# Prompt attention of a hybrid decoder step: TensorE's order of transposes and values product

## The chip, the cores and the metric

The kernel runs on one core of a Trainium2 chip. The metric is the time of one execution on the device in microseconds (us), from repeated runs. A profiled execution gives a trace of every instruction. The engines are TensorE (PE; PEld is its weight load), VectorE (DVE), ScalarE (ACT), GpSimd (POOL) and SyncE (SP); each works through its own instructions in order, and they wait for each other on semaphores.

## The reference

One inference step of a decoder layer. A prompt of 512 tokens and 8 sampled sequences of 8 tokens each, width 1024, go through a norm, one input projection, attention with 8 heads (2 key/value groups of 4 heads, head width 64) beside a pooling branch, an output projection and an MLP of width 4096. Everything is float32. Attention has three branches with their own keys and values: compressed blocks, selected blocks and a sliding window, mixed by gates. The part that this document is about is the prompt's:

```python
s = jnp.einsum('btgpd,bsgd->btgps', q, kv[..., 0, :]) * SCALE
s = s - slopes[None, None, :, :, None] * dist[None, :, None, None, :]
p = masked_softmax(s, mask)
o = jnp.einsum('btgps,bsgd->btgpd', p, kv[..., 1, :])
...
o = gates[0] * o_c + gates[1] * o_s + gates[2] * o_w
```

With 512 tokens in 8 blocks of 64, the 16 selected blocks are all blocks, so the selected branch is causal attention over the prompt, as is the window branch (window 512).

## The kernel before

The kernel is a sequence of blocks, each with one program per engine, and a block starts when the engines are through with the one before: projection and compression, prompt attention, attention of the samples, MLP. In the trace, prompt attention's main loop lies at about 247 to 332 us.

Prompt attention runs over 4 passes j, one for each head of a group (both groups' heads of that number are done together). A pass has U = 8 units: for each of 4 tiles of 128 queries, widest first, two branches (selected, window). A unit of tile i has scores of 128 queries against 128(i+1) keys, for two heads: widths of 512, 512, 384, 384, 256, 256, 128, 128. A unit goes through these stages:

- `scores` on TensorE (L1297) into two banks, two units in turn
- `sums` on VectorE (L1194): adds the distance penalty, takes the maximum, negates it (L1199)
- `exponent` on ScalarE (L1131), with the row sums
- `factors` on VectorE (L1204, L1208): one over the sum, times the gate
- the product with the factors on GpSimd (L1120); in the first two passes a page load for the samples' attention (L336) follows each of units 1 to 16
- `turn` on TensorE (L1312): 4(i+1) transposes of 64 rows into banks 4 and 5
- `keep_turned`: VectorE (L1212) copies bank 4 and ScalarE (L1137) copies bank 5 into a buffer `cpT`, of which there are two
- `values` on TensorE (L1327): 4(i+1) matmuls that add into bank 6; for the window branch, four more of the compressed branch (L1333)

Scores are issued AHEAD = 4 units before the values. The order on each engine is written out by hand in `body`. VectorE's step u is `keep_turned(u + 1)`, `sums(u + 4)`, `factors(u + 3)`; in steps 3 and 4 it also stages the next pass's queries (L1168) and penalties (L1173), and at a pass's end the factor of the compressed values (L1180), for which it waits until the pass's last values product is done. ScalarE's step is `keep_turned(u + 1)`, `exponent(u + 4)`, and at a pass's end a copy of bank 6 into `mixT` (L1145), for which the next pass's first values product waits.

`turn(u + 1)` waits for GpSimd's product of unit u + 1 and for both copies of unit u. `values(u)` waits for both copies of unit u. `scores(u + 4)` waits for the sums of unit u + 2.

Of the kernel before, what the change touches and what calls it, by code (L numbers as in the profile page):

```python
# [307 lines left out]
def const(m, name):  # L308
    a, n = m.ccols[name]
    return m.consts[:, a:a + n]  # L310
# [12 lines left out]
def values_at(m, i, br, n=P):  # L323
    return m.rowsT[0:n, i, KV * (br + 1) + P:KV * (br + 2)]
# [753 lines left out]
def prompt(nc, m, sems, sem):  # L1078
# [28 lines left out]
    with nc.Block() as block:  # L1107
        @block.sync
        def _(sp):
            for b in range(4):  # L1110
                load_window(sp, m, b, b, sems)
# [175 lines left out]
        @block.tensor  # L1287
        def _(pe):
            def scores(j, v):
                i, w = tile(v), width(v)  # L1290
                if v % U in (0, 4):
                    pe.wait_ge(q_staged, (j + v // U) * 2 + (1 + (v % U) // 4))
                if v >= 2:
                    pe.wait_ge(summed, j * U + (v - 1))
                for g in range(2):
                    a = HD * g
                    last = pe.matmul(pb[2 * (v % 2) + g][:, 0:w], m.qst[a:a + HD, P * i:P * i + P],  # L1297
                                     m.kT[a:a + HD, branch(v), 0:w], start=True, stop=True)
                last.then_inc(scored, 1)

            def turn(j, v):
                pe.wait_ge(scaled, j * U + (v + 1))
                if v >= 1:
                    pe.wait_ge(kept_dve, j * U + v)
                    pe.wait_ge(kept_act, j * U + v)
                n = tile(v) + 1
                for g in range(2):
                    for k in range(n):
                        to = 64 * (n * g + k)
                        for h in range(2):  # L1310
                            half = slice(64 * h, 64 * h + 64)
                            last = pe.transpose(pb[4 + h][:, to:to + 64], m.cp[v % 4][half, g, P * k:P * k + P],  # L1312
                                                ident[half, half])
                last.then_inc(p_turned, 1)

            def values(j, u):
                i, br = tile(u), branch(u)
                pe.wait_ge(kept_dve, j * U + (u + 1))
                pe.wait_ge(kept_act, j * U + (u + 1))
                if u == 0:  # L1320
                    pe.wait_ge(o_kept, j + 1)
                if u == 1:
                    pe.wait_ge(vst_staged, j + 1)
                out = lambda g: pb[6][HD * g:HD * g + HD, P * i:P * i + P]
                for k in range(i + 1):
                    for g in range(2):
                        last = pe.matmul(out(g), values_at(m, k, br)[:, HD * g:HD * g + HD],  # L1327
                                         m.cpT[u % 2][:, :, 64 * ((i + 1) * g + k):64 * ((i + 1) * g + k) + 64],
                                         start=(br == 0 and k == 0), stop=False,
                                         skip_group_check=True)  # L1330
                if br == 1:
                    for g in range(2):
                        last = pe.matmul(out(g), m.vst[0:64, HD * g:HD * g + HD], m.ccT[0:64, P * i:P * i + P],  # L1333
                                         start=False, stop=True, skip_group_check=True)
                if u == U - 1:
                    last.then_inc(o_done, 1)

            def body(j, last):
                for u in range(U):
                    values(j, u)  # L1340
                    if not last or u + 1 < U:
                        turn(j, u + 1)
                    if not last or u + AHEAD < U:
                        scores(j, u + AHEAD)

            scores(0, 0)
            scores(0, 1)
            pe.wait_ge(kc_ready, 1)
            for i in range(PTILES):
                for j in range(HPG):  # L1350
                    a = 64 * i + 16 * j
                    last = pe.matmul(pb[7][:, a:a + 16], m.qT[:, j, P * i:P * i + P], m.kc2, start=True, stop=True)
            last.then_inc(c_scored, 1)
            pe.matmul(pb[6][0:64, 0:P], const(m, "spread8")[0:PBLK, :], m.vc[0:PBLK, NB_SEQ, :], start=True, stop=True)\
              .then_inc(c_scored, 1)
            for v in range(2, AHEAD):
                scores(0, v)
            pe.wait_ge(c_ready, 2)
            for i in range(PTILES):
                last = pe.transpose(pb[7][0:64, P * i:P * i + P], m.cc[:, 64 * i:64 * i + 64], ident)  # L1360
            last.then_inc(c_turned, 1)
            pe.sem_inc(o_kept, 1)
            turn(0, 0)
            pe.wait_ge(vst_staged, 1)
            for j in range(HPG):
                body(j, j == HPG - 1)
# [746 lines left out]
```

## Time and profile before

| | us |
|---|---|
| median of three runs | 936.3 |
| lowest and highest | 934.24, 938.38 |
| profiled execution | 931.72 |
| its span, first to last instruction | 929.9 |
| mean granted TensorE clock, share of full | 0.953 |

The page gives the busy time of each engine over the span, a clock row in 40 slices of 23 us each, and groups of instructions with the idle time in front of them. Terms of a sum are taken from the profiled execution and compared with its own time.

### The profile page before, as it was taken

Reading aid. Unit: us, or ns where it says so; the run is one execution under the profiler, and the core shown is the slowest. Engines: PE = TensorE matmul, PEld = TensorE weight load, DVE = VectorE, ACT = ScalarE, POOL = GpSimd, SP = SyncE. Lnnn points to the kernel's source line nnn. Section 1 sums busy time; section 2 is a strip of 40 time slices with the busy share of each in tenths; the row PEclk is TensorE's granted clock in tenths of the full one; section 3 lists DMA queues with packets and bytes.
Section 4 is the critical chain, followed back from the end, with each engine's and each line's share of the span. In section 5 each row is a group of like instructions: output and inputs, shape, how many; then the busy total and the mean of one; then the engine's idle time right before and its main releaser. Section 6 shows DMA issues by size and latency. Waiting matters only on the chain.

```text
span 929.9 us, 16973 instructions
## 1 busy us (share of the span) xinstructions
PE 838.3 (90%) x7066; PEld 757.7 (81%) x7066; DVE 440.6 (47%) x971; ACT 334.5 (36%) x608; POOL 122.4 (13%) x119
## 2 busy tenths in 40 slices
PE   5999988877777787898899999999999999999994
PEld 4999966764544454566899999999999999999993
DVE  5335545645677756663535543244333442343324
ACT  6501054542355555453424441123211331133203
POOL 0000101100486424441020000000000000000000
PEclk8999999997699978999899999999999999999998
DMA  8912636841254020556420222222112222222002
GB/s 286 333 51 92 189 75 219 278 147 60 77 183 136 2 80 4 223 227 151 145 89 2 91 90 91 90 90 79 50 56 86 90 90 90 90 90 90 0 0 102
DMA packets 48782, 102.72 MB, mean 110 GB/s; under 512 B 7498, under 2 KB 19166, under 8 KB 46429
## 3 DMA queue, kind: packets, MB, share of 16 engines
q1 hardware_dynamic: 41821, 68.48, 22.2%
q0 software_dynamic: 6912, 33.56, 10.4%
q8 instruction: 35, 0.57, 0.3%
q14 instruction: 14, 0.11, 0.0%
HBM read 97.62 MB, written 8.53 MB: 114 GB/s over the span
## 4 chain that ended last, share of the span: by engine, by line
PE 50%; DVE 1%; ACT 1%; issue 0%; DVEq 0%; ACTq 0%
PE bank L1987 50%; DVE low L1974 1%; ACT low L1900 0%; DVE wl L1913 0%; PE bank L2029 0%; ACT wh L1856 0%; ACT small L1906 0%; DVE small L1971 0%; DVE hT L1926 0%; DVE hT L1951 0%; DVE xl L1930 0%; ACT low L1870 0%; DVE xl L1919 0%; ACT xh L1872 0%; DVEq L1810 0%
## 5 line engine op out<-in xcount | busy, mean ns | idle before, releaser
L1987 PE MATMUL bank<-xh,wh 128*128 128x288 f32 x640 | 138.2, 298 | 4.3 <-DVE xl L1919 3.9
L1987 PE MATMUL bank<-xl,wh 128*128 128x288 f32 x640 | 138.0, 297 | 0.0
L1987 PE MATMUL bank<-xh,wl 128*128 128x288 f32 x640 | 137.9, 297 | 0.0
L1856 ACT ACTIVATE wh<-low 128x1024 fp32r<-128x1024 f32 x72 | 75.1, 1050 | 121.3 <-PE bank L1987 121.0
L1987 PE MATMUL bank<-ah,wl 128*128 128x288 f32 x512 | 109.7, 296 | 0.0
L1987 PE MATMUL bank<-ah,wh 128*128 128x288 f32 x512 | 109.6, 296 | 0.0
L1987 PE MATMUL bank<-al,wh 128*128 128x288 f32 x512 | 109.6, 296 | 0.0
L1987 PEld LDWEIGHTS bank<-xh,wh 128*128 128x128 f32 x640 | 104.0, 190 | 5.0 <-DVE wl L1913 4.2
L1987 PEld LDWEIGHTS bank<-xl,wh 128*128 128x128 f32 x640 | 104.1, 190 | 0.0
L1987 PEld LDWEIGHTS bank<-xh,wl 128*128 128x128 f32 x640 | 103.9, 190 | 0.0
L1951 DVE TENSOR_TENSOR hT<-bank,hT 128x288 f32<-128x288 f32 x64 | 26.3, 453 | 138.9 <-PE bank L1987 138.9
L1913 DVE TENSOR_TENSOR wl<-low,wh 128x1024 fp32r<-128x1024 f32 x72 | 87.5, 1217 | 2.4 <-ACT wh L1856 2.4
L1987 PEld LDWEIGHTS bank<-ah,wh 128*128 128x128 f32 x512 | 82.5, 189 | 0.0
L1987 PEld LDWEIGHTS bank<-al,wh 128*128 128x128 f32 x512 | 82.5, 189 | 0.0
L1987 PEld LDWEIGHTS bank<-ah,wl 128*128 128x128 f32 x512 | 82.5, 189 | 0.0
L1883 ACT ACTIVATE tmp<-tmp 128x576 f32<-128x576 f32 x32 | 22.0, 686 | 152.2 <-DVE tmp L1947 152.2
L1947 DVE SCALAR_TENSOR_TENSOR tmp<-bank,norm 128x288 f32<-128x288 f32 x64 | 26.3, 454 | 103.6 <-PE bank L1987 103.4
L948 DVE TENSOR_TENSOR blkl<-bank,blkh 128x512 fp32r<-128x512 f32 x64 | 40.5, 684 | 25.3 <-ACT blkh L906 25.3
L1131 ACT ACTIVATE zone<-zone,small 128x512 f32<-128x512 f32 (+3 forms) x64 | 35.4, 554 | 41.9 <-DVE small L1199 40.5
L1327 PEld LDWEIGHTS bank<-zone,rowsT 128*64 128x64 f32 x320 | 18.4, 142 | 36.7 <-DVE zone L1212 29.3
L906 ACT ACTIVATE blkh<-bank 128x512 fp32r<-128x512 f32 x64 | 34.3, 597 | 34.5 <-PE bank L1012 34.5
L1327 PE MATMUL bank<-zone,rowsT 128*64 128x128 f32 x320 | 25.8, 290 | 23.1 <-ACT zone L1137 9.6
(323 smaller groups left out, 1375.2 us busy)
## 6 DMA issues: line engine op xcount, KB each, us to landing
low<-in_w_up SPq DMA_DIRECT2D x8, 2048.0 KB, 8.2
low<-in_w_down SPq DMA_DIRECT2D x8, 2048.0 KB, 7.8
zone<-in_cmp_w SPq DMA_DIRECT2D x16, 256.0 KB
o_swin<-in_state_win SPq DMA_DIRECT2D x8, 504.0 KB
px<-in_x_prompt SPq DMA_DIRECT2D x4, 512.0 KB, 5.4
u_raw<-in_w_in SPq DMA_DIRECT2D x1, 2048.0 KB, 10.0
q_raw<-in_w_in SPq DMA_DIRECT2D x1, 2048.0 KB, 10.4
low<-in_state_win SPq DMA_DIRECT2D x4, 512.0 KB
```

What stands on the lines that cost most here:

```text
L906: act.activation(m.blkh[u % RING][:, r, :], pb[4 + 2 * (u % 2) + r][:, :], ACT.Copy).then_inc(blk_hi, 1)
L948: dve.tensor_tensor(m.blkl[u % RING][:, r, :], pb[4 + 2 * (u % 2) + r][:, :], m.blkh[u % RING][:, r, :].bitcast(F32), ALU.subtract).then_i ...
L1131: last = act.activation(m.cp[v % 4][:, g, 0:width(v)], m.cp[v % 4][:, g, 0:width(v)], ACT.Exp, bias=nm(v)[:, g:g + 1], accum_out=su(v)[:, ...
L1327: last = pe.matmul(out(g), values_at(m, k, br)[:, HD * g:HD * g + HD], m.cpT[u % 2][:, :, 64 * ((i + 1) * g + k):64 * ((i + 1) * g + k) + 64],
L1856: act.activation(wcols(m.wh, i), raw_cols(i), ACT.Copy).then_inc(wh_ready, 1)
L1883: act.activation(m.act[i % 2], m.relu[i % 2], ACT.Square).then_inc(a_ready, 1)
L1913: dve.tensor_tensor(wcols(m.wl, i), raw_cols(i), wcols(m.wh, i).bitcast(F32), ALU.subtract)\
L1947: op = dve.scalar_tensor_tensor(out=half(m.relu[i % 2], hf), in0=out(i, hf), scalar=0.0, in1=half(m.rb, hf), op0=ALU.max, op1=ALU.mult)
L1951: op = dve.tensor_tensor(h, out(i, hf), h, ALU.add)
L1974: last = dve.scalar_tensor_tensor(out=m.yo[i][0:n, 512 * hf:512 * hf + 512], in0=pb[2 * (i % 4) + hf][0:n, :], scalar=yv(i)[0:n, :], in1=m ...
L1987: last = pe.matmul(out(i, hf), w[wi], half(x[:, k, :], hf), start=first and part == 0, stop=end and part == 2)
```

## The change

TensorE's step issues `turn(u + 1)` in front of `values(u)` where it issued it behind. The waits in both functions stay as they are; no other engine's program changes.

```diff
             def body(j, last):
                 for u in range(U):
-                    values(j, u)
                     if not last or u + 1 < U:
                         turn(j, u + 1)
+                    values(j, u)
                     if not last or u + AHEAD < U:
                         scores(j, u + AHEAD)
```

## Rows read from the trace of the kernel before

**Rows 1.** The page: span, busy time, and clock in 40 slices.
```profile
span 929.9 us, 16973 instructions
...
PE 838.3 (90%) x7066; PEld 757.7 (81%) x7066; DVE 440.6 (47%) x971; ACT 334.5 (36%) x608; POOL 122.4 (13%) x119
...
PEclk8999999997699978999899999999999999999998
```

**Rows 2.** Waits, 247 to 335 us: us in total, times, longest.
```profile
PEld bank L1327 <- DVE zone L1212: 29.3, 28, 1.8
POOL zone L1120 <- DVE small L1208: 28.6, 20, 4.8
...
DVE zone L1212 <- PE bank L1312: 17.4, 19, 3.1
```

**Rows 3.** A group by form, same stretch: busy us, mean ns | idle before.
```profile
L1327 PE MATMUL bank<-zone,rowsT 128*64 128x128 f32 x320 | 25.8, 290 | 23.1 <-ACT zone L1137 9.6 <-DVE zone L1212 8.0 <-ACT mixT L1145 3.0
```

**Rows 4.** One pass, values to values, by windows: length, then busy time.
```profile
293.53:315.45 21.92, 16.22 (x209) 10.12 (x209) 17.27 (x79) 12.88 (x41) 10.46 (x9) 1.00 0.04 17
```

**Rows 5.** Timeline of a step in mid-pass: start, us, instruction.
```profile
298.11 1.47 POOL L1120 TENSOR_TENSOR zone<-zone,small 128x768 f32<-128x768 f32 x1 [2.02 <-DVE small L1208]
...
299.45 0.88 PE L1327 MATMUL bank<-zone,rowsT 128*64 128x128 f32 x12 [0.19 <-DVE zone L1212]
...
300.26 0.59 PE L1312 MATMUL bank<-consts,zone 64*128 64x64 f32 x12
...
300.68 0.44 PE L1297 MATMUL bank<-kT,zone 64*128 64x128 f32 x4
...
300.89 0.56 DVE L1212 COPY zone<-bank 128x384 f32<-128x384 f32 x1 [0.23 <-PE bank L1312]
...
301.37 0.28 DVE L1194 CUSTOM_DVE_ANT_0 zone<-zone,bank 128x128 f32<-128x128 f32 x1
```

**Rows 6.** Timeline of the third boundary between passes.
```profile
311.08 1.89 POOL L1120 TENSOR_TENSOR zone<-zone,small 128x1024 f32<-128x1024 f32 x1 [1.73 <-DVE small L1208]
...
312.49 0.44 PE L1327 MATMUL bank<-zone,rowsT 128*64 128x128 f32 x4 [0.98 <-ACT zone L1137]
...
313.23 0.71 PE L1312 MATMUL bank<-consts,zone 64*128 64x64 f32 x16
...
313.77 0.86 PE L1297 MATMUL bank<-kT,zone 64*128 64x384 f32 x4
313.98 0.69 DVE L1212 COPY zone<-bank 128x512 f32<-128x512 f32 x1 [0.61 <-PE bank L1312]
...
314.70 0.55 DVE L1194 CUSTOM_DVE_ANT_0 zone<-zone,bank 128x384 f32<-128x384 f32 x1
```

**Rows 7.** Timeline of the first boundary: transposes and their copy.
```profile
268.45 0.72 PE L1312 MATMUL bank<-consts,zone 64*128 64x64 f32 x16
...
269.73 0.69 DVE L1212 COPY zone<-bank 128x512 f32<-128x512 f32 x1 [1.14 <-PE bank L1312]
```

**Rows 8.** Timeline of the last pass's end.
```profile
326.78 0.61 POOL L1120 TENSOR_TENSOR zone<-zone,small 128x256 f32<-128x256 f32 x1 [1.55 <-DVE small L1208]
...
327.77 0.66 PE L1327 MATMUL bank<-zone,rowsT 128*64 128x128 f32 x8 [0.80 <-ACT zone L1137]
327.83 0.61 POOL L1120 TENSOR_TENSOR zone<-zone,small 128x256 f32<-128x256 f32 x1 [0.43 <-DVE small L1208]
...
328.72 0.34 PE L1312 MATMUL bank<-consts,zone 64*128 64x64 f32 x4
...
329.10 0.29 DVE L1212 COPY zone<-bank 128x128 f32<-128x128 f32 x1 [1.35 <-PE bank L1312]
...
330.69 0.69 PE L1327 MATMUL bank<-zone,rowsT 128*64 128x128 f32 x4 [0.46 <-DVE zone L1212]
```

**Rows 9.** Timeline of the first step: transposes and their copy.
```profile
249.62 1.12 PE L1312 MATMUL bank<-consts,zone 64*128 64x64 f32 x16
...
250.78 0.69 DVE L1212 COPY zone<-bank 128x512 f32<-128x512 f32 x1 [3.12 <-PE bank L1312]
```

## The prediction
> **What bounds the kernel now.** I read the page first: one core, TensorE busy 90% of a 929.9 us span, and from about 500 us on nearly without a gap [rows 1]. The change touches only prompt attention, about 247 to 332 us. There the page's clock row, one digit to 23 us, shows the granted clock near its upper level with small dents. So next I asked for the waits of that stretch, engine by engine. TensorE's large wait is in front of the values product, L1327: its weight loads sat idle 29.3 us in 28 waits until VectorE's copy out of the transposes' banks (L1212) was done, and its matmuls 23.1 us [rows 2, 3]. VectorE in turn waited 17.4 us for the transposes. In this stretch no wait of TensorE was released by GpSimd: a product of GpSimd's (L1120) has always landed before its transposes get their turn. VectorE is busy 17.27 us of a 21.92 us pass [rows 4].
>
> I write, for one of the 32 units n: V(n) the values product, T(n) its transposes, K(n) the two copies, S(n) scores, X(n) VectorE's sums, F(n) the factors, E(n) ScalarE's exponent, P(n) GpSimd's product. Step n on TensorE is now V(n), T(n+1), S(n+4); on VectorE it is K(n+1), X(n+4), F(n+3), in that order. P(n+3) follows F(n+3).
>
> The timeline of one step in mid-pass is the key reading [rows 5]. Here n is 18. V(18) starts at 299.45, T(19) at 300.26, S(22) at 300.68 and ends at 301.12. K(19) starts at 300.89 and ends at 301.45; X(22) starts at 301.37. So the copy already runs beside the scores, and both end within 0.3 us of each other. The idle time in front of V is what is left of a ring: VectorE can't take X(n+4) before S(n+4) is done, and takes K(n+2) only after X(n+4) and F(n+3).
>
> **The change part by part.** Nothing is added or removed: the same 320 values matmuls (25.8 us) [rows 3], the matmuls of the compressed branch and the transposes are issued, with the same waits. T(n+1) moves in front of V(n). Both wait for K(n), so T can start where V starts now. No DMA and no queue of another engine is moved. V(n) and, behind it, S(n+4) now stand behind T(n+1), which also waits for P(n+1).
>
> 1) Middle of a pass. If P(n+1) is there, V and T swap places and S(n+4) starts when it does now. Only the copy is early, by the length of V. X(n+4) then starts after S instead of after K. For n = 18: S ends 301.12; X starts 0.06 later, as it does in [rows 6] (S 313.77 + 0.86 = 314.63, X 314.70), so at 301.18 instead of 301.37: a gain of 0.19 us. The next step, where both copies are narrower, gives some 0.06 by my reading; the steps of 512 and of narrow units around a pass's end give nothing, since X waits for S or for VectorE's own staging there. That is 0.25 us a pass, 1.0 us over four passes. The other bound is in the same rows: P(19) ends at 298.11 + 1.47 = 299.58, later than the 299.45 at which V(18) starts. Taking 0.1 us to see it, T(19) would start at 299.68, V(18) 0.42 later (T to S now), S another 0.81 later (V to T now), 300.91: ends 301.35, X 301.41, a loss of 0.04 us. If P also comes earlier, because its X did, the gain stands. I take the gain, and keep the loss for the range.
>
> 2) The boundary of two passes. Step 23 [rows 6]: V(23) starts at 312.49, T(24) at 313.23, S(27) at 313.77, X(27) at 314.70. P(24), the widest product, lands only at 311.08 + 1.89 = 312.97. T(24) can then start at 313.07, V(23) at 313.07 + 0.54 = 313.61, S(27) at 313.61 + 0.73 = 314.34. S starts 0.57 us later than now, and X(27), which starts at S's end even now, moves by 0.57 us. Behind it on VectorE stand F(26), the staging of the values factor and K(25), so the whole pass moves. At the two earlier boundaries GpSimd issues a page load behind each product, and the copy K starts 1.28 us after T (268.45 to 269.73) [rows 7] against 0.75 us here (313.23 to 313.98). This 0.53 us is a cushion: S may slip by it before it, not the copy, holds X. There I take 0.1 us each. The sum is 0.57 + 0.1 + 0.1 = 0.8 us lost. Bounds: 0.3 us if the gains of 1) bring P(24) forward too, 1.7 us if the cushion isn't one.
>
> 3) The end of the last pass, where there is no S left to hide a copy [rows 8]. Now: V(29) 327.77, T(30) 328.72, K(30) 329.10 to 329.39, V(30) 0.13 after that, 329.52, T(31) one short V later, 329.89, V(31) 330.69. Changed: T(30) starts at 327.77 (its product landed at 326.78 + 0.61 = 327.39) and takes some 0.20; V(29) runs 327.97 to 328.92; P(31) landed at 327.83 + 0.61 = 328.44, so T(31) starts at 328.92, V(30) at 329.12; K(31) starts 0.38 after T(31), as K(30) after T(30), and ends 329.59; V(31) starts at 329.72. That is 0.97 us earlier. A bound below is 0.5 us, if each copy's wait is only half hidden; above, 1.5 us, if V(31) also runs at the upper clock (0.44 instead of the 0.69 us of [rows 8], for it and for the pair behind it).
>
> The block after this one starts when all engines are through, so what is won or lost here reaches the end whole.
>
> Sum: -1.0 (1) + 0.8 (2) - 1.0 (3) = -1.2 us; since the loss of 1) is not unlikely I round it to -1.0. The profiled execution took 931.7 us beside its span of 929.9; it becomes 930.7. The median of the runs shown, 936.3, lies 4.6 above it; less 1.0 it is 935.3. No change is within 0.5%, 4.7 us, which is about what a measurement of this kernel can tell from none (the three runs span 934.24 to 938.38).
>
> **The rivals.**
>
> A: the copies are what bounds the pass. Then every wait of VectorE for the transposes goes, 17.4 us [rows 2] less the 3.1 us of the first one [rows 9], in which TensorE ran at its lower clock: 14 us, 922 us; half of it 929. For it: 28 of 28 waits in front of V name a copy. Against it: [rows 5], where scores end as the copy does, and VectorE's 17.27 us of work a pass, which leaves at most 4.65 us a pass whatever TensorE does. It needs X to start well before S ends, which it can't. The Trainium skill, Perfetto Trace Analysis, section Optimizing Tensor Performance, says that independent matmul groups should rotate through banks so that one group's evacuation lies beside the next group's matmuls; by that rule this order, which puts V between T and its copy's reader, should pay, and the time would be the 922 to 929 us of this rival. The trace bears it out only at the pass's end.
>
> B, slower: GpSimd's product becomes the wait in front of T, and holds V and S with it. Two steps of the ring S, X, F, P, T, S then have V(n) inside them, which now stands outside. Each step whose product lands later than K(n) by over about 0.1 us loses up to the length of V: 0.57 us at the boundary. Over the 28 steps that have scores, 0.2 us each is 5.6 us (941.9); 0.3 us is 8.4 (944.7). It decides from the point where products land 0.3 us later than now in most steps, for instance if GpSimd's signal reaches TensorE slower than VectorE's. For it: in [rows 5] the product is already 0.13 us behind. Against it: the gain in the same step offsets it, and GpSimd waits for VectorE 28.6 us [rows 2], so it isn't itself full.
>
> C: the clock. TensorE's order and its pauses change, so a stretch at 1.2 GHz could be longer or shorter. At the lower level sixteen transposes take 1.12 us [rows 9] against 0.71 [rows 6], and four values matmuls 0.69 [rows 8] against 0.44 [rows 6]; a step costs some 1.4 us more. Three steps either way are 4.2 us. For it: the clock falls right at the end of this part, at V(31). Against: the page's clock row shows nine tenths or more in the three slices from 256 to 325 us [rows 1], pauses and all.
>
> D: nothing moves at all, the gain of 3) included: 936.3.
>
> **How the numbers follow.** Forecast 0.64, A 0.11, B 0.12, C 0.08, D 0.05. Faster by over 0.5% is 0.8 of A and a quarter of C: 0.11. Slower by over 0.5% is 0.7 of B and a quarter of C: 0.10. Within: 0.79. The forecast's own range, from its bounds (-2.5 to +1.2 us) and 2 us of scatter, is 932 to 939. The range takes in the near halves of A to C: 930.5 to 940.
>
> **What would show it.** In the profile after: T(n+1) starts where V(n) started; the copies L1212 begin earlier against S, and TensorE's idle time in front of L1327 falls, to be found again in front of the transposes, L1312, with GpSimd named as releaser, above all at the boundaries. The pass lengths (22.6 and 21.9 us) stay within 0.3 us. The last three steps together are some 1 us shorter than now. The forecast is wrong if passes shorten by over 1 us (A), if T's waits for GpSimd sum to over 5 us beyond what V's waits lose (B), or if the clock row changes (C).

## The result, and the profile after

The changed kernel is slower. In the first comparison, 20 runs of each, its median is 938.5 us against 932.7 (ratio 1.0058, 95% interval 1.0035 to 1.0081); in a second, 12 runs against 35, it is 936.2 against 934.1 (1.0036, 0.9997 to 1.0075), which alone wouldn't tell it from no change. Medians are of all executions, ratios of those within 1.5% of the fastest of their kernel. The forecast was 1 us faster, within 0.5%.

The page of its profiled execution:

```profile
span 932.3 us, 16973 instructions
...
PE 841.7 (90%) x7066; PEld 757.9 (81%) x7066; DVE 440.4 (47%) x971; ACT 333.0 (36%) x608; POOL 122.6 (13%) x119
...
PEclk8999989988699998899799999999999999999998
```

The instruction counts are the same as in [rows 1]. The span says little here: two executions of the kernel before have spans of 929.9 and 935.8 us, because the stage ahead of prompt attention ends anywhere between 238 and 251 us and the samples' attention behind it takes 111 to 116 us, whatever is done in between. So I read all runs by a length inside the trace: **prompt attention**, from the start of its first copy L1212 to the start of the last copy L1145. Before it is 86.4 and 87.1 us in two profiles, changed 88.7 and 88.8. And within it by a middle pass, from one copy L1145 to the next, where the windows show the clock (third number from the end) at 1.00. Columns: window, length, then TensorE, its weight loads, VectorE, ScalarE, GpSimd. The kernel before, second profile:

```profile
273.38:295.94 22.56, 16.23 (x208) 10.12 (x208) 17.43 (x79) 13.16 (x43) 17.96 (x17) 1.00 0.56 187
295.94:318.25 22.31, 16.69 (x206) 10.75 (x208) 17.05 (x79) 13.00 (x43) 10.98 (x9) 0.95 0.06 23
```

The changed kernel, first profile:

```profile
272.19:295.42 23.23, 17.21 (x212) 10.61 (x208) 17.50 (x79) 12.77 (x43) 17.99 (x17) 0.99 0.63 183
295.42:318.55 23.13, 18.11 (x210) 11.42 (x208) 17.44 (x79) 12.65 (x42) 10.61 (x9) 0.93 0.06 21
318.55:335.44 16.89, 13.03 (x180) 8.81 (x176) 10.29 (x51) 8.15 (x29) 6.89 (x7) 1.00 0.01 2
```

and second profile:

```profile
292.40:315.12 22.72, 16.81 (x210) 10.60 (x208) 17.45 (x79) 12.65 (x43) 10.63 (x9) 1.00 0.06 22
```

The first middle pass (with page loads) goes from 22.57 and 22.56 us in the two profiles of before to 23.23, +0.66 us. The second (without) goes from 21.9 [rows 4] to 22.72, +0.8 us. The last pass got shorter, 17.34 to 16.89 us, although its part ahead of the last steps is some 1.0 us longer. A fall of the clock at the edge of a pass costs it another 0.4 us (22.31 against 21.92; 23.13 against 22.72); in the second profile of the changed kernel one cost its first middle pass 0.8 us (24.00 against 23.23, mean clock 0.94).

The waits of the changed kernel, 247 to 340 us:

```profile
PEld bank L1312 <- POOL zone L1120: 26.9, 23, 2.2
DVE zone L1194 <- issue: 12.5, 19, 1.2
PE bank L1312 <- ACT zone L1137: 7.0, 8, 1.3
PE bank L1312 <- POOL zone L1120: 6.3, 8, 1.6
DVE zone L1212 <- PE bank L1312: 6.0, 9, 1.3
```

Against [rows 2]: the wait in front of the values product is gone. One of 26.9 us stands in front of the transposes, and the profile names GpSimd's product. VectorE's wait for the transposes fell from 17.4 to 6.0 us, and one of 12.5 us in front of its sums came up, which was 1.1 us in 3 waits before. That is the copy coming early and the sums then standing still for scores. By this list the product is the culprit. In part the list is right: in 12 of the steps the transposes start 0.05 to 0.06 us after the product has landed, and 0.3 to 0.9 us after the later of the two copies, 7.7 us in sum. Whether that is what the kernel loses by, the list can't say; the experiments say that the loss comes without it, too.

The timeline of the same step as in [rows 5], unit 18, in the changed kernel:

```profile
301.48 1.47 POOL L1120 TENSOR_TENSOR zone<-zone,small 128x768 f32<-128x768 f32 x1 [2.01 <-DVE small L1208]
...
303.00 0.59 PE L1312 MATMUL bank<-consts,zone 64*128 64x64 f32 x12 [0.18 <-POOL zone L1120]
...
303.52 0.88 PE L1327 MATMUL bank<-zone,rowsT 128*64 128x128 f32 x12
...
304.13 0.55 DVE L1212 COPY zone<-bank 128x384 f32<-128x384 f32 x1
...
304.32 0.49 PE L1297 MATMUL bank<-kT,zone 64*128 64x128 f32 x4
...
304.87 0.28 DVE L1194 CUSTOM_DVE_ANT_0 zone<-zone,bank 128x128 f32<-128x128 f32 x1 [0.19 <-issue]
```

Before, from the start of TensorE's step to the end of its scores: 299.45 to 301.12, 1.67 us. Now 303.00 to 304.81, 1.81 us, for the same three pieces of work. Transposes to values takes 0.52 us and values to scores 0.80; before, values to transposes took 0.81 and transposes to scores 0.42. The scores' own row is 0.49 instead of 0.44 us. TensorE pays 0.14 us a step for the order alone, and all of it lies in front of the end of the scores. It is so in the other steps of a pass, too, wherever nothing waits inside the step: 1.41 became 1.55 us, 1.91 became 2.06, 2.15 became 2.30, 2.21 became 2.35, 2.47 became 2.61. In this step the sums start 0.06 us behind the scores' end.

The end of the last pass, against [rows 8]:

```profile
332.06 0.36 ACT L1137 ACTIVATE zone<-bank 128x256 f32<-128x256 f32 x1
...
332.56 0.34 PE L1312 MATMUL bank<-consts,zone 64*128 64x64 f32 x4 [1.25 <-ACT zone L1137]
...
332.83 0.66 PE L1327 MATMUL bank<-zone,rowsT 128*64 128x128 f32 x8
...
334.17 0.29 DVE L1212 COPY zone<-bank 128x128 f32<-128x128 f32 x1 [0.94 <-PE bank L1312]
...
335.44 0.60 ACT L1145 ACTIVATE mixT<-bank 128x512 f32<-128x512 f32 x1 [1.00 <-PE bank L1333]
```

From ScalarE's copy of unit 29 to the last copy L1145 it is 3.38 us, where it was 4.80 (327.26 to 332.06). In the second profile of the kernel before, whose last steps ran at the upper clock, it was 4.28. The kernel before, first and second profile:

```profile
327.26 0.36 ACT L1137 ACTIVATE zone<-bank 128x256 f32<-128x256 f32 x1
...
332.06 0.60 ACT L1145 ACTIVATE mixT<-bank 128x512 f32<-128x512 f32 x1 [1.51 <-PE bank L1333]
```

```profile
331.72 0.36 ACT L1137 ACTIVATE zone<-bank 128x256 f32<-128x256 f32 x1
...
336.00 0.60 ACT L1145 ACTIVATE mixT<-bank 128x512 f32<-128x512 f32 x1 [0.99 <-PE bank L1333]
```

### The profile page after: what moved, and what is told of

It reads as the page before. It is cut to its first block, busy times and chain, and to the rows that moved or that the text cites. A ratio compares the mean times of both kernels' runs of the same rounds, so it can differ in the third digit from the quotient of the medians.

```text
span 932.3 us, 16973 instructions
## 1 busy us (share of the span) xinstructions
PE 841.7 (90%) x7066; PEld 757.9 (81%) x7066; DVE 440.4 (47%) x971; ACT 333.0 (36%) x608; POOL 122.6 (13%) x119
## 4 chain that ended last, share of the span: by engine, by line
PE 50%; DVE 1%; ACT 1%; issue 0%; DVEq 0%; ACTq 0%
PE bank L1987 50%; DVE low L1974 1%; ACT low L1900 0%; DVE wl L1913 0%; PE bank L2029 0%; ACT wh L1856 0%; ACT small L1906 0%; DVE small L1971 0%; DVE hT L1951 0%; DVE hT L1926 0%; DVE xl L1930 0%; ACT low L1870 0%; DVE xl L1919 0%; ACT xh L1872 0%; DVEq L1810 0%
## 5 line engine op out<-in xcount | busy, mean ns | idle before, releaser
L948 DVE TENSOR_TENSOR blkl<-bank,blkh 128x512 fp32r<-128x512 f32 x64 | 40.6, 684 | 26.9 <-ACT blkh L906 26.9
L1120 POOL TENSOR_TENSOR zone<-zone,small 128x1024 f32<-128x1024 f32 (+3 forms) x32 | 40.7, 1272 | 45.3 <-DVE small L1208 44.9
L1029 PE MATMUL bank<-blkh,w1h 64*128 64x512 f32 x128 | 31.1, 476 | 15.1 <-DVE blkl L948 14.9
```

The source lines that it names most:

```text
L948: dve.tensor_tensor(m.blkl[u % RING][:, r, :], pb[4 + 2 * (u % 2) + r][:, :], m.blkh[u % RING][:, r, :].bitcast(F32), ALU.subtract).then_i ...
L1029: last = pe.matmul(pb[c][:, :], w, x, start=u == 0 and q == 0 and part == 0, stop=u == UNITS - 1 and q == 1 and part == 2)
L1120: pool.tensor_tensor(m.cp[v % 4][:, :, 0:width(v)], m.cp[v % 4][:, :, 0:width(v)], su(v).unsqueeze(2).broadcast_to([P, 2, width(v)]), ALU. ...
```

## The experiments

The theories that the expectations name. Product: the transposes, now in front, wait for GpSimd's product and hold values and scores back. Queue: ScalarE's copy stands behind an exponent in its queue, so early transposes gain nothing. Changeover: TensorE's order costs some 0.15 us a step in front of the scores, and late scores are what a pass pays for. Clock: the runs differ by where the clock falls. Noise.

**The changed kernel again.**

> The changed kernel once more, as the yardstick for the runs beside it, and for a second profile. Product theory (transposes in front wait for GpSimd's product and hold the values product and the scores back): slower again by 2 to 6 us, the three pass boundaries losing some 0.7 us each and the last steps winning 1 us. Clock theory (the difference of the two kernels comes from stretches at 1.2 GHz that fall differently): the pass lengths differ from the first profile's by over 1 us and follow the clock row; the ratio may come out at 1.00. Noise theory: ratio 1.000 within 0.003.

Measured: 1.0036 (0.9997 to 1.0075), prompt attention 88.8 us. The passes repeat the first profile's but for the clock, so noise and clock don't make the difference inside prompt attention.

**Values first at the boundary only** (edit of the changed kernel).

```diff
+                    if u == U - 1:
+                        values(j, u)
                     if not last or u + 1 < U:
                         turn(j, u + 1)
-                    values(j, u)
+                    if u < U - 1:
+                        values(j, u)
```

> Transposes first in all steps but the last of each pass, where the values product goes first as in the kernel before. Product theory: the three boundary waits of 1.55 us in front of the transposes, each of which cost some 0.7 us, are gone, so it is 1.5 to 2.5 us faster than the changed kernel, and still slower than before by the 0.2 us of the steps between. Clock theory: no difference to the changed kernel that the boundary explains.

Measured: 934.6 us (ratio to before 1.0006, 0.9964 to 1.0048), prompt attention 89.7 us, with a clock fall in it. Its first middle pass, at the upper clock throughout:

```profile
267.80:291.04 23.24, 17.09 (x208) 10.56 (x208) 17.68 (x79) 12.78 (x43) 18.01 (x17) 1.00 0.60 181
```

23.24 us against 23.23. Putting the values product first at the boundary, where the wait was longest, gave nothing in this pass; the 0.66 us are lost in the steps between. The gain of 1.5 to 2.5 us that the product theory wanted didn't come in the trace, and the medians (1.6 us apart) can't tell.

**Transposes first only at the very end** (edit of the kernel before).

```diff
+                    early = last and u >= U - AHEAD
+                    if not early:
                         values(j, u)
                     if not last or u + 1 < U:
                         turn(j, u + 1)
+                    if early:
+                        values(j, u)
```

> The kernel before, with transposes first only in the last four steps of the last pass, where no scores follow. Product theory: the last steps are 1.0 us shorter, all else as before, so 1 us faster than before (ratio 0.999). Clock theory: the end of this part falls differently against the clock's low stretch behind it, so the blocks after it may move by up to 4 us either way.

Measured: 930.5 us, 0.9968 (0.9930 to 1.0006). Prompt attention 86.2 us against 86.4, with one more clock fall in its profile (its second middle pass is 22.36 us instead of 21.9 for it), and the last pass 16.87 against 17.34 us. From ScalarE's copy of unit 29 to the last copy L1145 it is 3.39 us, as in the changed kernel, against 4.80 and 4.28 in the two profiles of before. So the gain at the end is there without the loss in the passes; the ratio alone doesn't prove it.

**Values last** (edit of the changed kernel).

```diff
                     if not last or u + 1 < U:
                         turn(j, u + 1)
-                    values(j, u)
                     if not last or u + AHEAD < U:
                         scores(j, u + AHEAD)
+                    values(j, u)
```

> The changed order with scores in front of the values product: transposes, scores, values. Product theory: the values product is out of the ring of scores, sums, factors, product and transposes altogether, in which it stood behind the transposes in the changed kernel; each step's scores come 0.4 to 1.4 us earlier, and the loop is then bound by VectorE's 17.3 us of work a pass: 1 to 2.5 us a pass shorter than before, 3 to 8 us in all, ratio 0.992 to 0.997. Rival (scores' place doesn't matter, the copies or the clock do): like the changed kernel, 1.002 to 1.008.

Measured: 927.8 us, 0.9946 (0.9910 to 0.9983), prompt attention 79.4 us. Windows of its middle passes:

```profile
272.07:292.94 20.87, 16.00 (x208) 9.82 (x204) 17.60 (x75) 12.78 (x41) 16.87 (x16) 1.00 0.63 185
292.94:313.26 20.32, 16.02 (x208) 10.03 (x208) 18.06 (x81) 12.78 (x42) 10.86 (x9) 1.00 0.06 23
```

1.7 and 1.6 us a pass shorter than before, with VectorE busy 84 and 89% of a pass. The transposes are in front of the values here too, as in the change. What differs from the change is only that the scores don't stand behind the values. The transposes still start right behind the product in 11 steps, 6.4 us after the later copy in sum, nearly as in the changed kernel, and prompt attention is 9 us shorter than there all the same. So the place of the scores is what counts, and such waits alone don't make a kernel slower than before.

**Half a product, in both orders.** GpSimd scales only the first half of each head's keys; the other half of the probabilities stays unscaled.

```diff
-                pool.tensor_tensor(m.cp[v % 4][:, :, 0:width(v)], m.cp[v % 4][:, :, 0:width(v)],
-                                   su(v).unsqueeze(2).broadcast_to([P, 2, width(v)]), ALU.mult).then_inc(scaled, 1)
+                w = width(v) // 2
+                pool.tensor_tensor(m.cp[v % 4][:, :, 0:w], m.cp[v % 4][:, :, 0:w],
+                                   su(v).unsqueeze(2).broadcast_to([P, 2, w]), ALU.mult).then_inc(scaled, 1)
```

> The kernel before, with GpSimd's product over only the first half of each head's keys (the other half of the probabilities is left unscaled); the products take about half as long. This run is read by the length of prompt attention in its profile (86.4 us in the kernel before, from the first copy L1212 to the start of the last copy L1145). No product is waited for in the kernel before, so: 85.5 to 86.5 us.

> The changed kernel (88.7 us by the same measure) with the same halved product. Product theory: with the product early, transposes first cost nothing any more, and prompt attention is 1 us shorter than in the order of before with the halved product. Queue theory (the loss comes from TensorE's change of instruction kinds in front of the scores, 0.2 us a step, and from ScalarE's copy, which stands behind its exponent and so gains nothing from early transposes): at least 1 us of the 2.3 us stays, 87.0 us or more.

> The kernel before with the halved product, once more: the two middle passes 20.9 us each within 0.2 where the clock is at its upper level.

> The changed kernel with the halved product, once more. If the loss belongs to the order: a middle pass at the upper clock is 21.5 us within 0.2. If it was the execution's: as with the order of before, 20.9.

Measured: prompt attention 81.5 and 81.4 us in the order of before, 85.5 and 84.3 changed. Middle passes, order of before (second profile):

```profile
274.27:295.19 20.92, 16.21 (x210) 10.12 (x208) 16.11 (x79) 12.88 (x43) 13.62 (x16) 1.00 0.66 201
295.19:316.11 20.92, 16.22 (x210) 10.12 (x208) 16.12 (x79) 12.88 (x43) 5.90 (x8) 1.00 0.06 23
```

and changed (second profile):

```profile
268.92:290.44 21.52, 16.82 (x210) 10.67 (x208) 16.09 (x78) 12.63 (x43) 13.66 (x16) 1.00 0.63 197
```

The first profiles gave 20.93 and 21.53 us for the first of these. In this pass no transposes start sooner than 0.35 us after their product has landed, and in seven of its eight steps a copy ends last; in the eighth the product lands 0.18 us after the copies, but TensorE is still busy then. So with the product half as long and waited for by none, transposes first costs 0.60 us a pass, against 0.66 with the whole one. The product theory, which wanted this loss gone, falls. The other forecast, 87.0 us or more, was a miss as well (85.5 and 84.3), since it was counted from the whole product. What this run can't say is how the 0.66 us of the whole-product kernel divide between the order and its waits for the product. Yet the waits of this kernel still say:

```profile
PEld bank L1313 <- POOL zone L1121: 20.0, 16, 1.7
...
PE bank L1313 <- ACT zone L1138: 10.8, 12, 1.3
```

(Its lines are one further down.) The transposes wait for the product and for both copies. One such wait in its timeline:

```profile
276.60 0.61 POOL L1121 TENSOR_TENSOR zone<-zone,small 128x256 f32<-128x256 f32 x1 [0.87 <-DVE small L1209]
...
277.18 0.47 ACT L1138 ACTIVATE zone<-bank 128x384 f32<-128x384 f32 x1
...
277.76 0.35 PEld L1313 LDWEIGHTS bank<-consts,zone 64*128 64x128 f32 x8 [1.18 <-POOL zone L1121]
277.79 0.47 PE L1313 MATMUL bank<-consts,zone 64*128 64x64 f32 x8 [1.02 <-ACT zone L1138]
```

The product had landed at 277.21; ScalarE's copy ended at 277.65, and the transposes went 0.1 us later. The weight load's row names GpSimd all the same; the matmuls' row names the copy. In the changed kernel with the whole product the name GpSimd is right in 12 steps, here it isn't. My expectation for the order of before was off by 4 us, too (81.5 instead of 85.5 to 86.5): a product that no one waits for is still in the ring, and it slows VectorE (last section).

**ScalarE's copy in front of its exponent, in both orders and with values last.**

```diff
                     if not last or u + 1 < U:
                         keep_turned(j, u + 1)
...
-                    if not last or u + AHEAD < U:
-                        exponent(j, u + AHEAD)
+                    if not last or u + AHEAD - 1 < U:
+                        exponent(j, u + AHEAD - 1)
```

> TensorE's order of the kernel before; on ScalarE the exponent of unit n+3 stands behind the copy of unit n+1, where it stood in front of it. It is the yardstick for the same edit with transposes first. Queue theory: the copy starts when the transposes end, 0.1 to 0.9 us earlier in the wide units, the exponent later, so that the factors may have to wait: prompt attention (86.4 us before) 84 to 88 us. Clock theory: nothing to tell.

> The changed kernel (transposes first) with the same edit on ScalarE. Queue theory (transposes first gain nothing because ScalarE's copy stands behind the exponent of unit n+3 and starts up to 1.6 us after them): now both copies follow the transposes at once, TensorE's next step starts right behind its scores, and prompt attention is at least 1 us shorter than in the changed kernel (88.7 us), and not more than 0.5 us longer than with the order of before and the same edit. Changeover theory (the loss lies in what TensorE issues in front of the scores, whatever ScalarE does): 1.5 to 2.5 us longer than with the order of before and the same edit.

> Transposes, scores, values in a step (prompt attention 79.4 us), with the copy in front of the exponent on ScalarE. Queue theory: the copies that started up to 1.5 us after their transposes start with them: 77 to 79 us. If instead the exponent is now the late one, the factors wait for it on VectorE and the products on GpSimd follow: 80 to 83 us.

Measured, to before: 1.0012 (0.9986 to 1.0038), 1.0012 (0.9977 to 1.0047) and 0.9991 (0.9967 to 1.0015). Prompt attention 87.3, 89.5 and 85.3 us. With ScalarE's copy freed of the exponent, transposes first still costs 2.1 us between one profile of each, as it did without (2.3); the ratios don't tell the two orders apart. The clock falls are several in these profiles, 0.91 and 0.90 on average, so I don't read single passes. The queue theory forecast at least 1 us less than the changed kernel's 88.7 us and got 0.8 more; as far as these two profiles go it falls as the cause. With values last the edit costs 5.8 us (79.4 to 85.3), more than either forecast allowed (77 to 79 and 80 to 83); how much of it is clock falls isn't known. There ScalarE waits 31.3 us for transposes in front of its copies, which was 4.2 us, and the exponents stand behind it; the matmul waits in front of the transposes that are put down to GpSimd grow from 7.0 to 12.4 us.

**Scores first, two ways.**

> The order scores, values, transposes in a step. Scores need no copy of this step, so they run while the copies do. If late scores are what both kernels pay for, this is faster than before by as much as the order with the values product last (6 us), since VectorE's sums never wait for TensorE; the transposes then stand behind both, at a loss of up to 0.9 us a step in front of the next copy: between 0 and 6 us faster. Rival (TensorE's order matters only by what stands in front of the transposes): slower than before by the scores' 0.45 to 1.1 us a step.

> Scores, transposes, values in a step. The scores wait for no copy of this step and nothing stands in front of them; the transposes come behind the scores, up to 1.1 us later than with transposes, scores, values. If VectorE's sums are what waits, prompt attention is 79 to 81 us as with values last; if the copies are, it is longer by the part of the scores that now lies between a copy and the next transposes, 0.3 us a step, 88 us.

Scores, values, transposes: 939.9 us, 1.0037 (0.9998 to 1.0075). Its forecast of 0 to 6 us faster was a miss. In its one profiled execution (949.1 us) the mean granted clock was 0.75 to 0.81 from pass to pass, so its lengths can't be set beside the others'. Scores, transposes, values: 927.2 us, 0.9939 (0.9911 to 0.9967), prompt attention 81.6 us, just above the 79 to 81 of its forecast. With values last it doesn't matter much which of the other two is first; with the transposes last the gain is lost. I take it that late transposes make the copies and so the next step late; no run shows it alone.

**The same small work in front of the scores and behind them**, in the order of before:

```diff
                     values(j, u)
                     if not last or u + 1 < U:
                         turn(j, u + 1)
                     if not last or u + AHEAD < U:
+                        for _ in range(4):
+                            pe.transpose(pb[7][:, 0:64], ident[0:64, :], ident[0:64, 0:64])
                         scores(j, u + AHEAD)
```

and, for the other, with the two new lines below `scores`.

> The kernel before with four more small transposes (64 by 64, of constants into a free bank) in front of the scores of each step; four such transposes take 0.15 to 0.2 us from start to the next instruction's start. Changeover theory: scores that come 0.15 to 0.2 us later cost a pass at the upper clock 0.5 to 0.8 us, as the changed order does: 23.1 to 23.4 and 22.4 to 22.7 us where the kernel before has 22.57 and 21.93. Rival (TensorE has slack there, since the copies end as the scores do): passes within 0.2 us of the kernel before.

> The kernel before with the same four small transposes behind the scores, where TensorE would else idle until the copies are done. Both theories: passes within 0.2 us of the kernel before; a loss here would say that the small work costs something other than its place.

Measured: 1.0020 (0.9983 to 1.0056) and 1.0019 (0.9987 to 1.0051); prompt attention 89.6 and 88.3 us. Here the medians say nothing and the passes everything. In front:

```profile
266.30:289.82 23.52, 18.15 (x240) 12.09 (x240) 17.71 (x79) 13.06 (x42) 17.97 (x17) 1.00 0.61 179
289.82:312.45 22.63, 17.98 (x240) 12.09 (x240) 17.41 (x79) 12.89 (x43) 10.60 (x9) 1.00 0.07 23
```

Behind, with clock falls in both of its middle passes:

```profile
272.62:295.60 22.98, 18.60 (x234) 13.47 (x236) 17.44 (x79) 13.11 (x43) 18.38 (x17) 0.93 0.62 188
```

In front, a pass is 0.95 and 0.70 us longer than before, all at the upper clock, without a change to any wait in the program. The changed order costs 0.66 and 0.8. But the padding puts the scores off by more than the change does. The step of [rows 5] in the padded kernel:

```profile
296.48 0.88 PE L1327 MATMUL bank<-zone,rowsT 128*64 128x128 f32 x12
...
297.96 0.44 PE L1297 MATMUL bank<-kT,zone 64*128 64x128 f32 x3
```

From its start to the end of the scores it is 1.92 us, against 1.67 before and 1.81 in the changed kernel: 0.25 us later, where the text above expected 0.15 to 0.2 and the change costs 0.14. Taken down in that proportion, 0.14 us a step would cost some 0.5 and 0.4 us a pass (an estimate from these two profiles). Behind, the first middle pass is 0.4 us longer, which is the price of a clock fall. Until the clock falls, its steps lie where those of before lie: counted from the copy L1145 that begins the pass, its first scores of 384 keys start at 18.25 us against 18.21; with the padding in front they start at 19.2.

## Why the prediction was wrong

**The reading of what bounds a pass was right, but not followed to its end.** The step at 299.45 was read as: copy and scores end within 0.3 us of each other, VectorE can't sum before the scores. Both hold; that is why 23 us of TensorE's idle time could move without a gain, and why rival A failed. But if the sums wait for scores, then anything that makes scores later is paid, and anything that leaves them in their place gains nothing. In the order of before and in the changed one both the values product and the transposes stand between the copies and the scores, so the swap could at best leave the scores where they were.

**Step 1 failed.** It said: "If P(n+1) is there, V and T swap places and S(n+4) starts when it does now." The gain was to be 0.25 us a pass. Measured is a loss of 0.66 and 0.8 us a pass. Swapping isn't free on TensorE: [rows 5] against the same step now give 0.14 us more to the end of the scores, and so do the other steps. This was a cost that the prediction put at nothing without a reason. The padded kernel showed that late scores are paid for in both middle passes, 0.95 and 0.70 us for 0.25 us a step. The halved product showed 0.60 us a pass with the wait for the product out of the way. What the waits for the product add in the whole-product kernel, between nothing and some 0.4 us a pass by the estimate above, stays open. The other bound that the step gave, 0.04 us lost through the product, had the right sign and not the right size, and lacked the cost of the order.

**Step 2** gave 0.8 us for three boundaries, 0.1 of it at each with page loads. With values first at the boundary the first middle pass stays at 23.24 us, which agrees with next to nothing for those. The 0.57 us of the third was not measured alone: the second middle pass of that run has a clock fall in it. The reading behind it holds: the scores there start 1.44 us after the product has landed, where they started 0.80 us after it before, 0.64 us more.

**Step 3 was right.** Forecast was 0.97 us. The last stretch is 1.42 us shorter, of which some 0.5 is the clock: the final values products and L1145's wait ran at the lower clock before (330.69 to 332.06, 1.37 us) and at the upper one now (334.56 to 335.44, 0.88). The remaining 0.9 is the hidden copies; the second profile of before, at the upper clock there, has 4.28 against 3.38 us, 0.90.

**The sum**: +3.7 us over the passes, -1.4 at the end, +2.3 us in prompt attention, where -1.0 was forecast. Some 0.4 of the first figure and 0.5 of the second are the clock. Rival B was on the right side, with part of the mechanism: the values product in the way of the scores. That products must land late for it, as B wanted, the halved product refutes, and the loss is some 0.1 us a step, not its 0.2 or 0.3. The clock, rival C, isn't the cause in the middle passes, which were compared at the upper clock.

**The range** held the number (938.5 us) only since before, with more runs, has a median 3.6 us lower than the 936.3 that it was counted from.

**Open.** The first comparison's interval begins at 3.3 us, the profiles show 2.3 us (1.6 against the second profile of before). Whether something outside prompt attention adds to it, or more frequent clock falls inside, isn't settled. Falls ahead of its last steps stand in all six profiles with the order transposes, values, scores, and in four of eight with the order of before; each costs a pass some 0.4 to 0.8 us, and so few profiles don't prove a difference. Why TensorE takes 0.14 us longer in the changed order isn't known either.

## What to carry to other kernels

Where one engine's wait has been found, look at what the engine behind it is doing at that moment: if the next thing that it needs is something else (here scores), filling the wait gains nothing, and the order should be changed so that this comes first. Here that meant putting the work that nobody waits for, the values product, last: 0.54% faster than before, by the same kind of edit. And measure an order's cost by padding: the same small work on either side of the suspected product tells which place is paid for. Read in the trace how late the padding really made things before setting its cost beside the change's.

A wait on several semaphores is named after one of them. Before building on the name, look in the timeline for which of them ended last, and shorten that work alone.

## What was unexpected of the hardware

GpSimd's product slows VectorE. The staging of the values factor (L1180, 64 by 64 elements in SBUF, two instructions a pass) takes 1197 ns on average in the kernel before between 268 and 320 us, and 530 ns with half the product. At the third boundary of the kernel before the first of the pair took 0.25 us; the second started at 316.47, when the product had just begun, and ended at 317.92, 0.05 us after the product. VectorE's busy time in the first middle pass falls from 17.43 to 16.11 us, and the middle passes from 22.57 and 21.93 to 20.92 us each. The pair and the product in the kernel before:

```profile
316.30 1.62 DVE L1180 TENSOR_SCALAR zone<-zone,consts 64x64 f32<-64x64 f32 x2
316.38 1.49 POOL L1120 TENSOR_TENSOR zone<-zone,small 128x768 f32<-128x768 f32 x1 [1.04 <-DVE small L1208]
```

The group in the kernel before, and in the halved kernel in the order of before, first profiles:

```profile
L1180 DVE TENSOR_SCALAR zone<-zone,consts 64x64 f32<-64x64 f32 x6 | 5.2, 1197 | 0.0
...
L1181 DVE TENSOR_SCALAR zone<-zone,consts 64x64 f32<-64x64 f32 x6 | 2.9, 530 | 0.0
```

The Trainium skill, SBUF — State Buffer, section Who interferes with whom, names tensor_scalar among the VectorE operations that can contend with GpSimd for the port pair that the two share; the trace agrees, with these numbers.

Transposes that run while GpSimd issues an indirect DMA are seen late by both engines that wait for them, VectorE and ScalarE. The boundary of the changed kernel where a page load follows the product:

```profile
293.48 0.71 PE L1312 MATMUL bank<-consts,zone 64*128 64x64 f32 x16 [1.56 <-POOL zone L1120]
...
293.57 0.98 POOL L336 DMA_INDIRECT zone<-in_cache_slc,idx_slc  x1
...
294.93 0.69 DVE L1212 COPY zone<-bank 128x512 f32<-128x512 f32 x1 [1.10 <-PE bank L1312]
```

Both copies start 1.45 us after the transposes, 0.38 us after the DMA's issue has ended. At the boundary without page loads the copy starts 0.76 us after them (316.86 to 317.62). In the kernel before it is 1.28 us [rows 7] against 0.75 [rows 6]. With half the product, order of before, the issue ends as the transposes start (268.52 and 268.50), and VectorE's copy starts 0.76 us after them, though a page load follows the product there too. So the delay goes with the issue running beside the transposes; what in it holds the copies isn't known, and no run tried it alone.
